# The latents' attention logits as three products of high and low parts, with the low parts cut by GpSimd

## The reference

```python
def attend(qblk):                       # q: 512 x 8 heads x 96, k: 768 x 8 heads x 96
    logits = jnp.einsum('bqhd,bkhd->bhqk', qblk, k).astype(jnp.float32) * SM_SCALE
    p = jax.nn.softmax(logits, axis=-1).astype(v.dtype)
    return jnp.einsum('bhqk,bkhd->bqhd', p, v)
# k: 64 columns of its own per head, and 32 columns (rotary) that all heads share
```

## Time and profile before

| | us |
|---|---|
| median of 3 runs | 2896.44 (2896.41 to 2896.81) |
| the profiled execution | 2895.06 |
| its span, first to last instruction | 2893.8 |
| PE busy in it | 2800.7 (97%) |
| PEld / DVE / POOL / ACT busy | 2309.8 / 1566.6 / 1341.7 / 1195.5 |
| granted TensorE clock, mean | 0.994 |

### The profile page before, as it was taken

One profiled execution on the slowest core, in us unless ns is written; L12 is line 12 of the kernel. 1 busy time (PEld: TensorE's weight loads), 2 busy tenths in 40 slices (PEclk: granted clock), 3 DMA queues, 4 the chain that ended last, 5 costly groups with the idle time before them and its releaser, 6 DMA issues.

```text
span 2893.8 us, 41021 instructions
## 1 busy us (share of the span) xinstructions
PE 2800.7 (97%) x16134; PEld 2309.8 (80%) x16134; DVE 1566.6 (54%) x2640; ACT 1195.5 (41%) x1985; POOL 1341.7 (46%) x869
## 2 busy tenths in 40 slices
PE   7889999999999999999999999999999999999999
PEld 6577778888888786778888787888878878888887
DVE  4448653246554475636554566676543567667432
ACT  4353554554434444544433544333433543333333
POOL 4253247874454442344554653434534733435344
PEclk9999999999999999999999999999999999999999
DMA  6834114558773324048673432111222421112223
GB/s 248 318 102 150 41 45 146 181 168 245 206 206 127 117 76 146 1 138 227 197 209 105 126 96 62 59 59 59 90 71 94 134 80 62 59 52 78 83 73 117
DMA packets 96431, 351.03 MB, mean 121 GB/s; under 512 B 10224, under 2 KB 10736, under 8 KB 94320
## 3 DMA queue, kind: packets, MB, share of 16 engines
q1 hardware_dynamic: 89616, 316.95, 33.2%
q0 software_dynamic: 6624, 31.46, 5.5%
HBM read 333.69 MB, written 2.10 MB: 116 GB/s over the span
## 4 chain that ended last, share of the span: by engine, by line
PE 79%; DVE 15%; ACT 3%; issue 2%; POOL 1%; DMA 0%; SPq 0%; POOLq 0%; ACTq 0%; DVEq 0%
PE ps L716 56%; PE ps L689 5%; DVE ps L2614 4%; PE ps L1103 3%; PE ps L897 3%; DVE t L2776 2%; PE ps L918 2%; DVE t L2759 1%; PE ps L744 1%; PE ps L1134 1%; PE ps L1197 1%; PE ps L1208 1%; PE ps L1022 1%; DVE t L2793 1%; PE ps L1375 1%
## 5 line engine op out<-in xcount | busy, mean ns | idle before, releaser
L716 PE MATMUL ps<-t,t 128*128 128x512 f32 (+3 forms) x8784 | 1953.8, 379 | 23.6 <-DVE t L2316 7.4
L716 PEld LDWEIGHTS ps<-t,t 128*128 128x128 f32 x8784 | 1561.5, 189 | 325.2 <-issue 36.8
L3363 POOL TENSOR_TENSOR t<-t,t 128x1024 fp32r<-128x1024 f32 (+1 forms) x452 | 1076.0, 2386 | 1001.2 <-ACT t L1526 928.6
L1526 ACT ACTIVATE t<-t 128x1024 fp32r<-128x1024 f32 (+1 forms) x452 | 463.7, 1030 | 760.8 <-PE ps L716 569.3
L689 PE MATMUL ps<-t,t 128*128 128x128 f32 (+2 forms) x1662 | 238.3, 278 | 26.6 <-DVE t L2523 4.8
L689 PEld LDWEIGHTS ps<-t,t 128*128 128x128 f32 (+2 forms) x1662 | 190.2, 141 | 73.1 <-ACT t L1675 16.6
L1103 PE MATMUL ps<-t,t 128*128 128x512 f32 x1008 | 232.3, 390 | 1.9 <-DVE t L2793 1.6
L1103 PEld LDWEIGHTS ps<-t,t 128*128 128x128 f32 x1008 | 188.2, 188 | 44.3 <-DVE t L2793 3.2
L2614 DVE SCALAR_TENSOR_TENSOR ps<-t,t,ps 128x512 f32<-128x512 f32 (+1 forms) x174 | 116.1, 667 | 6.4 <-ACT ps L1783 0.6
L3383 POOL TENSOR_TENSOR t<-t,t 128x4 f32<-128x4 f32 (+2 forms) x96 | 86.6, 902 | 59.8 <-DVE t L2320 27.4
L2759 DVE TENSOR_TENSOR t<-t,t 128x1024 fp32r<-128x1024 f32 x42 | 85.0, 2025 | 51.9 <-ACT t L1910 51.9
(11 more groups left out here) (293 smaller groups left out, 2814.3 us busy)
## 6 DMA issues: line engine op xcount, KB each, us to landing
t<-in_wbig SPq DMA_DIRECT2D x412, 512.0 KB, 3.5
t<-in_wmod SPq DMA_DIRECT2D x96, 512.0 KB, 6.2
t<-in_wbig SPq DMA_DIRECT2D x24, 1024.0 KB, 8.2
t<-in_wbig POOLq DMA_DIRECT2D x18, 1024.0 KB, 13.9
t<-t POOLq DMA_DIRECT2D x12, 1024.0 KB, 11.0
t<-in_wbig SPq DMA_DIRECT2D x16, 416.0 KB, 3.2
t<-in_wbig SPq DMA_DIRECT2D x16, 332.0 KB, 2.9
t<-in_wbig SPq DMA_DIRECT2D x14, 256.0 KB, 2.7
```

Of the source, the lines that this page charges most:

```text
L716: m = p.matmul(out, lhs, rhs, start=kk == 0 and n == 0, stop=kk == tiles - 1 and n == 2)
L1526: a.activation(c.hi(w), c.raw(w), ACT.Copy).then_inc(w_hi.h, w_hi.up(("cut", w)))
L3363: g.tensor_tensor(c.lo(w), c.raw(w), c.hi(w).bitcast(F32), ALU.subtract).then_inc(w_lo.h, w_lo.up(("cut", w)))
```

## The change

In l0 and l1 the logits are made of three float32r products instead of one float32 product: QTH·KTH + QTH·KTL + QTL·KTH. ScalarE writes the high parts `QTH` (from PSUM, beside the copy into `QT`) and `KTH` (from `KT`) into the unused tail of the constants; GpSimd subtracts them from `QT` and `KT` in place, and the results are `QTL` and `KTL`. For that, `rows2` moves behind the constants in memory and is loaded with the late constants. The shared 32 key rows are copied from PSUM into both `KT` buffers at the start of the stage, where there was one copy from PSUM and one from `KT[0]` in head 1. The context's attention (c0) stays as it was.

```diff
+        lows, _ = self.row(early, [[96, 768]] * 2 + [[96, 512]] * 2, F32R)
+        self.KTL, self.QTL = lows[0:2], lows[2:4]
...
+        highs, a = self.row(tail, [[96, 768]] * 2 + [[96, 512]] * 2, F32R)
+        self.KTH, self.QTH = highs[0:2], highs[2:4]
...
 pe_program, load_head(h):
-            free[at], free[at + 1] = ((act, ("qt", n, h)),), ((dve, ("ktr", n, h, 0)),)
+            free[at], free[at + 1] = ((act, ("qh" if rope else "qt", n, h)),), ((dve, ("ktr", n, h, 0)),)
...
 pe_program, logits(u):
             P.wait_ge(act, ("qt", n, h))
             P.wait_ge(dve, ("kt", n, h))
+            if rope:
+                P.wait_ge(pool, ("ql", n, h))
+                P.wait_ge(pool, ("kl", n, h))
             for j in range(2):
                 k0, kn = j * nh, min(nh, nk * 128 - j * nh)
+                if rope:
+                    parts = (c.QTH, c.KTH), (c.QTH, c.KTL), (c.QTL, c.KTH)
+                    for m_, (q, k) in enumerate(parts):
+                        m = p.matmul(Q[:, 512 * j:512 * j + kn], q[b][:, 128 * t:128 * t + 128], k[b][:, k0:k0 + kn],
+                                     start=m_ == 0, stop=m_ == 2)
+                    continue
...
 act_program, attention:
+            if n[0] == "l":
+                a.activation(c.QTH[h % 2][:, 0:128 * nt], c.pair(("head", n, h))[0:96, 0:128 * nt], ACT.Copy).then_inc(
+                    act.h, act.up(("qh", n, h)))
+
+        def keys(h, part):
+            rows, cols = 64 if h > 1 else 96, slice(512, 768) if part else slice(0, 512)
+            A.wait_ge(dve, ("kt", n, h) if part or not h else ("ktr", n, h, 0))
+            a.activation(c.KTH[h % 2][0:rows, cols], c.KT[h % 2][0:rows, cols], ACT.Copy).then_inc(
+                act.h, act.up(("kh", n, h, part)))
...
         load_head(0)
+        if n[0] == "l":
+            keys(0, 0)
+            keys(0, 1)
         n_u = NH * nt
         for u in range(n_u + 5):
+            ahead = u // nt + 1 if n[0] == "l" and u // nt + 1 < NH else None
+            if ahead and u % nt == 3:
+                keys(ahead, 1)
             if u < n_u:
                 logits(u)
             if 1 <= u <= n_u:
                 turn(u - 1)
+            if ahead and u % nt == 2:
+                keys(ahead, 0)
...
 dve_program, load_rest(h):
-                    v.tensor_copy(c.KT[0][64:96, 128 * k0:128 * (k0 + kn)],
-                                  c.bank(("kr", n, k0))[64:96, 0:128 * kn]).then_inc(
-                        dve.h, dve.up(("ktr", n, "r", k0), ("kt", n, h)))
-            if h == 1:
+                    for K in c.KT if n[0] == "l" else c.KT[0:1]:
+                        v.tensor_copy(K[64:96, 128 * k0:128 * (k0 + kn)],
+                                      c.bank(("kr", n, k0))[64:96, 0:128 * kn]).then_inc(
+                            dve.h, dve.up(("ktr", n, "r", k0), ("kt", n, h)))
+            if h == 1 and n[0] == "c":
...
 pool_program, attention:
+        def queries(h):
+            G.wait_ge(act, ("qh", n, h))
+            g.tensor_tensor(c.QTL[h % 2][:, :], c.QT[h % 2][:, :], c.QTH[h % 2][:, :].bitcast(F32), ALU.subtract).then_inc(
+                pool.h, pool.up(("ql", n, h)))
+
+        def keys(h, part):
+            rows, cols = 64 if h > 1 else 96, slice(512, 768) if part else slice(0, 512)
+            G.wait_ge(act, ("kh", n, h, part))
+            g.tensor_tensor(c.KTL[h % 2][0:rows, cols], c.KT[h % 2][0:rows, cols],
+                            c.KTH[h % 2][0:rows, cols].bitcast(F32), ALU.subtract).then_inc(
+                pool.h, pool.up(("kl", n, h)))
+
+        if n[0] == "l":
+            queries(0)
+            keys(0, 0)
+            keys(0, 1)
         n_u = NH * nt
         for u in range(n_u + 5):
+            ahead = u // nt + 1 if n[0] == "l" and u // nt + 1 < NH else None
+            if ahead and u % nt == 2:
+                queries(ahead)
+                keys(ahead, 0)
+            if ahead and u % nt == 3:
+                keys(ahead, 1)
             if n_u - nt + 3 <= u < n_u + 3:
                 finish(u - 3 - n_u + nt)
...
             next(tail, None)
             yield
...
 sp_program: rows2 is loaded behind the late constants
```

More of the change, by code:

```diff
@@ L517, in memory @@
         self.WX = [self.row(a - 4096 * NS * w, [[128, 1024]] * NS)[0] for w in (2, 1)]
-        (self.K, self.cols2, self.rows2, self.half, self.st, self.st2, self.hgb), a = self.row(
-            a, [[128, NCC], [128, L, NC2], [128, L, NR2], [128, 16], [128, 64], [128, 64], [128, L, 24]])
+        (self.K, self.rows2, self.cols2, self.half, self.st, self.st2, self.hgb), a = self.row(
+            a, [[128, NCC], [128, L, NR2], [128, L, NC2], [128, 16], [128, 64], [128, 64], [128, L, 24]])
         two = a
@@ L572, in memory @@
         w += self.row(tail, [[128, 2, 1024]])[0]
+        highs, a = self.row(tail, [[96, 768]] * 2 + [[96, 512]] * 2, F32R)
+        assert a <= tail + 4 * (NCC - self.CC["ut"][0]) + 4 * L * NR2
+        self.KTH, self.QTH = highs[0:2], highs[2:4]
         self.WN = dict(zip(WN_SUM, w))
@@ L775, in prep @@
         else:
-            P.wait_ge(*((c.s["ctx"], 16) if n == "c0" else (c.s["inputs"], 64)))
+            P.wait_ge(*((c.s["ctx"], 16) if n == "c0" else (c.s["inputs"], 48)))
         for k in ks[0:2]:
@@ L1396, in layer @@
         if i == 0:
-            P.wait_ge(c.s["late"], 16)
+            P.wait_ge(c.s["late"], 32)
         n = f"d{i}"
@@ L1561, in squares @@
         if n == "l0":
-            A.wait_ge(inputs, 64)
+            A.wait_ge(inputs, 48)
         for t in range(nt):
@@ L2183, in layer @@
         if i == 0:
-            A.wait_ge(c.s["late"], 16)
+            A.wait_ge(c.s["late"], 32)
         def sm(b):
@@ L3248, in layer @@
         if i == 0:
-            V.wait_ge(c.s["late"], 16)
+            V.wait_ge(c.s["late"], 32)
         def out(s, b):
@@ L3297, in dve_program @@
     next(rest)
-    V.wait_ge(inputs, 64)
+    V.wait_ge(inputs, 48)
     g = prep("l0")
@@ L3722, in layer @@
         if i == 0:
-            G.wait_ge(c.s["late"], 16)
+            G.wait_ge(c.s["late"], 32)
         second = prep_pair(f"d{i}", 1)
@@ L3758, in pool_program @@
     next(rest)
-    G.wait_ge(inputs, 64)
+    G.wait_ge(inputs, 48)
     steps = prep("l0")
@@ L3860, in sp_program @@
                 c.s["late"].h, c.s["late"].landed())
+            s.dma_start(c.rows2[:, :, :], src["rows2"]).then_inc(c.s["late"].h, c.s["late"].landed())
         elif kind == "const":
@@ L3863, in sp_program @@
             s.dma_start(c.cols2[:, :, :], src["cols2"]).then_inc(inputs.h, inputs.landed())
-            s.dma_start(c.rows2[:, :, :], src["rows2"]).then_inc(inputs.h, inputs.landed())
         else:
```

## The result

The changed kernel takes 2944.06 us (median of 4 runs, 2941.28 to 2946.56); the kernel before took 2896.43 beside it. The ratio is 1.0168, with a 95% interval of 1.0156 to 1.0181: slower by 48 us, where 2938 was forecast (range 2914 to 2955). The profiled execution took 2945.3 us, 50.2 more than that of before.

The account below looks back on a forecast made before the run. PE was taken as the bound, busy 97% of the span, with DVE and ACT latency limiting slots without `valued`. Terms -12.0 + 7.7 + 32.8 + 13.3 = +41.8 gave 2938 us, range 2914 to 2955.

Parts of the forecast that it names:

- The four terms: Both stages together: shorter products -12.0 us, later stage starts +7.7, waits in odd heads +32.8, falls of the clock +13.3.
- the largest term: The waits of PE in heads 1, 3, 5 and 7 of both stages, +32.8 us.
- Odd heads: First logits wait for GpSimd's low keys behind the tail: 5.1 us each in heads 5, 7; 3.1 in 1, 3.
- Even heads: Heads 2, 4, 6: no tail in the way, low parts ready with 0.3 us to spare, so no wait.
- Starts: At each stage's start the first logits come 3.8 us later, behind key-row copies and cuts; +7.7 us in both.
- The clock: PE's clock falls behind long idles in the two stages: eight falls of 1.66 us, +13.3 us.
- The products: Six float32r products take 1.08 us instead of 1.38 per unit's logits, gaining 0.30; 12 us in both stages.
- I cost these at nothing: Extra work per head, ACT about 1.6 us and DVE a little less, and one more late-constants DMA: no cost.
- 768 records: Expected in the profile after: the new logits line L908 with 768 records at about 0.18 us each.

Follow-up runs that it names:

- Experiment 1: Changed kernel with GpSimd's low part of a head's last 256 keys moved directly behind the first piece, ahead of the tail's three operations; 2916.02 us.
- Experiment 5: Changed kernel with head 0 of each stage in plain float32, without cuts, and the shared key rows copied to its buffer first; 2930.26 us.
- Experiment 2: Changed kernel with PE multiplying the unit matrix by itself ahead of each of the ten waits; 2934.23 us.
- experiment 9: Kernel before with each unit's two float32 products replaced by six float32r ones over unchanged tiles, no cuts, no waits; 2886.74 us.
- Experiment 4: Changed kernel with plain float32 products again, cuts still made, and PE's two waits on GpSimd removed; 2911.29 us.
- experiments 6 and 7: 6: changed kernel with the next head's loading one slot earlier on all engines, 2924.67 us; 7: the same plus head 0 in plain float32, 2912.12 us.

## Why the prediction was right, and where it was not

The forecast's sum was +41.8; 50.2 came between the profiled executions. From the stage's first transposes to its projection l0 grew from 120.08 to 144.93 us and l1 by 24.9, so 49.8 of the 50.2 lie in the two stages. The four terms that the forecast priced were short or too hopeful by 0.2 to 5 us each, all on the same side, and none of them cancelled another. What made the number good is that the largest term was right.

- *Odd heads:* right, by the chain as it was followed. The high part of the first 512 keys ended at 4.57 after logits(18) (4.38 expected), their low part at 5.90 (5.75), the tail at 8.73 (8.63), the next logits came at 9.55 (9.5). The losses in l0 are 5.12 twice, 3.19 (unit 4) and 3.05 (unit 12), and in l1 the same within 0.01: 33.0 in both stages for 32.8. Experiment 1 moved the instruction that the chain names, and units 4, 12, 20 and 28 then start 6.7 us after the unit two before, where it was 9.6: less by 2.8, the time of the tail's three operations.
- *Even heads:* right. Units 8, 16 and 24 have no wait; unit 24 came 0.28 earlier after unit 22, not 0.61.
- *Starts:* 4.2 and 4.1 instead of 3.8, 8.3 for 7.7. The chain left out ACT's second copy of the queries, for which PE waits 0.81 us where it waited 0.33. Experiment 5 takes away start and fall together and gains 10.7 us by the times, 13.8 in the stages.
- *The clock:* 13.3 was forecast as eight falls of 1.66. There were nine at the ten waits, from 0.69 to 2.74 us each by the rows. Experiment 2, which removes the falls and leaves the waits, shows 15.5 in the stages and 9, known to some 6, in the times. By the stages that is 1.7 per fall. The rule of the Trainium skill ("TensorE: Matmul & The Clock Gate", section "HAM oscillation — how this bites in real kernels"), by which bursts behind waits start at the low clock, held in this trace at nine waits; the exception is the wait of 2.99 us before unit 12 of l0. Behind the same wait in l1 the clock fell.
- *The products:* this term failed in its size. "So six take 1.08 us, and a unit gains 0.30 us of PE" subtracts six spacings of records inside long runs from 1.38 us, which is a distance to the next instruction. The spacing was right (0.175 here, for 0.180). But the four float32 records alone take 1.29 us; the other 0.09 of the 1.38 is the step to `valued`, and it stays with six products. The first of the six takes 0.26 us to the second, 0.09 more than the others, and wins 0.08 back by starting sooner. So a unit gains 0.22, and not all of it arrives: outside the stretches of starts and odd heads the two stages of experiment 9 are 7.0 us shorter (8.2 with them), where the forecast had 12.0. This is most of what the forecast missed. The Trainium skill's formula ("TensorE: Matmul & The Clock Gate", section "Back-to-back issue gap") gives 0.1625 us per product and lies further off still, and its gain of 0.41 per unit is nowhere in the runs. What makes up the 0.09 us at either end (the change of kind, or the first weights) no run tells.
- *"I cost these at nothing"* for ACT's additional work: wrong as a step, though without effect on the sum. Experiment 4, with the cuts and copies but no wait for a low part, is 17 us over the kernel before, some 12 of its 20 in the stages at the late tail. In the changed kernel the same delay of the tail lies inside PE's longer wait, as row L1767 shows with 2.53 us of waiting for the same operation; it comes out as soon as the longer wait is taken away: PE's waits of 1.25 us in experiment 1 and of 1.6 in experiments 6 and 7 stand behind the same tanh, and are part of why these stayed above the kernel before. How much of it they are was not measured alone. The argument that ACT idles 2.27 us before an exponential looked at how much time ACT has, not at whom it stands behind.
- *Records:* "768 records" for L908 was a miscount; 64 units of six are 384. Their busy time over count is 96.8/384 = 0.25 us, not 0.18; it holds the stretches at the low clock and the longer first and last record of each unit.

Sum with the measured sizes: -7.0 + 8.3 + 33.0 + 15.5 = 49.8, against 49.8. That it closes to a tenth is luck, since every term is read from one execution.

## What to carry to other kernels

A product that is split into cheaper ones is paid by whoever makes the parts: follow the parts through every engine's order up to the first product that needs them, and count what is queued in front of them. Then ask what the parts, put in front, now delay: here an engine with half its time free made PE wait through an operation three links away. And before such a change, price the gain in its own place, between its real neighbours, from the start of one slot to the next; the run with the products alone shows 0.23%, and no version tried here paid for the cuts of all heads out of that.

## What the runs showed of the hardware

- Inside a run a float32r product of 96x384 (contraction by columns) came every 0.175 us, and a float32 product, two records of 0.322, every 0.64. Three for one saves 0.12 us per half. A unit of six float32r products between float32 ones takes 1.24 us to `valued` and 1.15 to transposes (two products: 0.53 and 0.44); the float32 pair of the same size 1.38 and 1.29. Counted from slot to slot the gain is 0.22.
- The clock fell behind every idle time of PE of 4.6 and 5.1 us. Behind 2.99 us (unit 12 of the changed kernel) it fell in l1 and not in l0, behind 2.23 us in three of four places of experiment 1, behind 2.05 us in all four of experiment 4, behind 1.6 us in l0 of experiment 6 and not in l1. Behind 3.22 us (unit 4 of l1 in experiment 5) it did not fall. The idle time alone does not tell. At the low level six products took 2.26 us for 1.29, less than double.
- A float32r output costs what a float32 one does: ACT's copies of 96x512 take 0.59 us to float32r (L1682) and 0.58 to float32 (L1679); GpSimd's subtraction of 64x256 takes 0.72 us with a float32r result, its float32 operations of 128x256 the same.
